# Decoder step on eight cores: first bands built during the x load, scores of the next unit ahead of each attention unit, other places for cache and output loads

## The chip, the cores and the metric

The kernel runs on the 8 cores of one Trainium2 chip. Each core has five engines that run their own instruction streams and wait for each other through semaphores: TensorE (PE, matmuls), VectorE (DVE), ScalarE (ACT), GpSimd (POOL) and SyncE (SP, which here only issues DMAs). All eight cores run one program on their own part of the data, without exchange. The time of a run is that of the slowest core, in device microseconds; the lower the better.

## The reference

One layer of a hybrid decoder, for a prompt of 4 x 2048 positions and 32 single decode positions, model width 2048:

```python
h = rms_norm(x, norm_mix_g);  z = h @ w_in       # q 1024 | k 256 | v 256 | GLU value 1024 | GLU gate 1024
q, k = rope(rms_norm(q)), rope(rms_norm(k))      # 16 query heads, 4 key/value heads of 64
a = attention(q, k, v, window 128, sink per head) # 128-blocks: own and previous key block; decode: cache
u = u_val * sigmoid(u_gate)                       # GLU
c = silu(layer_norm(causal_dwconv(u, width 31)))  # per channel; layer_norm over 1024 channels
x = x + concat([a, c]) @ w_out
x = x + square(relu(rms_norm(x) @ w_up)) @ w_down # hidden 8192
# returned beside x: the last keys, values and GLU rows of prompt and decode (caches shifted by one)
```

## The kernel before, in words

Each core has half a prompt (1024 positions, plus a halo of 128 for keys and convolution) and 4 decode positions. Everything is held transposed: channels on the 128 partitions, positions along the row. `Prog.add` keeps one instruction list per engine in the order of the calls and derives the semaphore waits from overlapping byte ranges and PSUM banks. So the order of the Python calls is the order on every engine, and each engine works strictly in that order. A DMA issued on POOL or SP also stands in that engine's list: its wait holds up all behind it.

**x load** (loop at L611). 16 chunks of x (`xu`, SP queue) come in; DVE scales each with the norm's gain into bf16 (`HT`, L612), ACT squares it, PE multiplies it with the first two weight blocks (gate and value of channel block 0) and sums the squares. The weights of the u projection (`load_wu`, 4 slots) come over POOL's queue.

**u blocks** (loop L835, c = 1 to 7). Per channel block of 128: `u_block` twice (gate in PSUM banks 0 to 2, value in 3 to 5, 48 matmuls each), `glu_gate` (DVE product, ACT sigmoid, POOL product with the norm), `glu_mul` (16 pieces on DVE, L681, into `UP`), `conv` (36 matmuls with banded matrices `BD`, banks 6 and 7, drained by ACT in 16 pieces, L706, into `CC`). `build_bands` (L657) makes the banded matrices from the taps `WT` on POOL, one product of 4608 columns per block, in two buffers. In the gaps, `kv_tile` projects a tile of keys and values (bank 6), chain1 and chain2 do norm and rotation on DVE, ACT and POOL, and `kv_tr` transposes the keys. For block 0, glu_mul's both inputs lie in SBUF, for the others one lies in PSUM.

**Passage** (from L1050). Last key tiles, q projection of the decode tile (9) and of tiles 1 and 2, the conv states (`u_outputs`, L868), the cache loads (`CKB`, `CVB`, L1064), and the first LayerNorm sums (`ln_cast`, `ln_stats`). In memory, the squares of `ln_cast` lie over the buffer `UTO` from which the conv state is sent out.

**Attention** (loop L1097, 8 blocks of 128 positions, two units of 8 heads each). `sc`: scores and mask, 8 matmuls in a ring of three banks, exps on ACT into `PT`; `pv`: sums and values, 8 matmuls in banks 7 and 6; `unit_b`: DVE adds the sink, ACT does Ln and Exp for the reciprocal, DVE multiplies. Between them stand quarters of the q projection three tiles ahead (`q_part`, banks 0 and 1), its norm and rotation (`q_chain1`, `q_chain2`), its transposes (`q_tr`), and the LayerNorm (`ln_norm1`, `ln_norm2`, per channel block: two DVE products of 1029 columns, then ACT's scaling of 1029 columns, L919). Sigmoids (`ln_sig`) and products (`ln_mul`) follow in blocks 5 and 6; each `ln_mul` is followed by the load of the residual chunk that goes into the same place.

**Output projection** (L1166 on) and **MLP** (64 hidden blocks): 16 output blocks of 48 matmuls, then groups of four up and 16 down blocks. Weights come over POOL's queue.

## Time and profile before

| | us |
|---|---|
| median of 3 runs | 1601.51 (1598.77 to 1603.36) |
| profiled execution | 1603.6 |
| its span, slowest core (core 7) | 1602.0 |
| spans of the eight cores | 1596.6 to 1602.0 |
| PE busy | 1406.0 (88% of the span) |
| DVE, ACT, POOL busy | 662.8, 389.3, 284.1 |

The share of PE is a mean over stages that differ: the page's 40 slices of 40 us show PE at nine tenths or more from slice 15 on and between five and seven tenths in most slices before, apart from slices 4 to 6. The clock of PE that the chip granted is full in the first and falls in the second. In the rows below, a line of the timeline gives the start, the length, the engine and line, and in brackets how long the engine stood idle before it and what ended that; xN means N instructions of this form in a row.

### The profile page before, as it was taken

Reading aid. Unit: us, or ns where it says so; the run is one execution under the profiler, and the core shown is the slowest. Engines: PE = TensorE matmul, PEld = TensorE weight load, DVE = VectorE, ACT = ScalarE, POOL = GpSimd, SP = SyncE. Lnnn points to the kernel's source line nnn. Section 1 sums busy time; section 2 is a strip of 40 time slices with the busy share of each in tenths; the row PEclk is TensorE's granted clock in tenths of the full one; section 3 lists DMA queues with packets and bytes.
Section 4 is the critical chain, followed back from the end, with each engine's and each line's share of the span. In section 5 each row is a group of like instructions: output and inputs, shape, how many; then the busy total and the mean of one; then the engine's idle time right before and its main releaser. Section 6 shows DMA issues by size and latency. Waiting matters only on the chain.

```text
span 1602.0 us, 22075 instructions; the slowest of 8 cores (1596.6 to 1602.0 us)
## 1 busy us (share of the span) xinstructions
PE 1406.0 (88%) x9006; PEld 869.2 (54%) x9006; DVE 662.8 (41%) x743; ACT 389.3 (24%) x536; POOL 284.1 (18%) x275
## 2 busy tenths in 40 slices
PE   5659997577655499999999999999999999999994
PEld 2436663222221366566666666666666666666663
DVE  2635555343433211115435435534443553453463
ACT  4256775154437122210100110010011011001000
POOL 0376652311211000010101110110010111011000
PEclk9879998778777799999999999999999999999997
DMA  9813431300001844484552553364355246336419
GB/s 253 161 27 53 81 60 39 32 26 0 1 0 53 208 77 71 68 137 73 92 81 45 86 92 55 65 106 67 53 92 91 44 78 99 58 62 100 66 35 177
DMA packets 52517, 122.75 MB, mean 77 GB/s; under 512 B 19215, under 2 KB 22543, under 8 KB 52395
## 3 DMA queue, kind: packets, MB, share of 16 engines
q0 software_dynamic: 43888, 91.07, 36.1%
q1 hardware_dynamic: 8531, 30.28, 7.0%
q8 instruction: 73, 1.20, 0.3%
q14 instruction: 25, 0.20, 0.0%
HBM read 203.42 MB, written 10.35 MB: 133 GB/s over the span
## 4 chain that ended last, share of the span: by engine, by line
PE 78%; DVE 5%; ACT 5%; DMA 4%; issue 3%; POOL 2%; SPq 1%; ACTq 0%; DVEq 0%; POOLq 0%
PE psum L535 78%; DVE arena L507 3%; ACT arena L503 3%; DMA arena<-cv 2%; DMA arena<-xu 2%; SPq L490 1%; POOL arena L507 1%; DVE arena L681 1%; DMA arena<-wo 1%; ACT L503 1%; ACT arena L706 0%; PE psum L539 0%; POOL arena L490 0%; POOL arena L522 0%; DVE arena L702 0%
## 5 line engine op out<-in xcount | busy, mean ns | idle before, releaser
L535 PE MATMUL psum<-arena 128*128 128x343 bf16 (+5 forms) x8880 | 1396.5, 320 | 147.5 <-ACT arena L503 86.2
L535 PEld LDWEIGHTS psum<-arena 128*128 128x128 bf16 (+1 forms) x8880 | 859.3, 99 | 676.0 <-issue 229.8
L507 DVE TENSOR_TENSOR arena<-psum,arena 128x1029 f32<-128x1029 f32 (+6 forms) x394 | 399.5, 1025 | 485.6 <-PE psum L535 420.3
L503 ACT ACTIVATE arena<-psum 128x1029 bf16<-128x1029 f32 (+6 forms) x157 | 117.5, 772 | 797.5 <-PE psum L535 790.2
L507 DVE TENSOR_TENSOR arena<-arena 128x1029 bf16<-128x1029 bf16 (+5 forms) x126 | 129.0, 1029 | 294.6 <-ACT arena L503 288.2
L507 POOL TENSOR_TENSOR arena<-arena 128x256 f32<-128x256 f32 (+7 forms) x74 | 172.8, 2338 | 408.7 <-DVE arena L507 164.9
L503 ACT ACTIVATE arena<-arena 128x1029 bf16<-128x1029 f32 (+13 forms) x201 | 142.0, 732 | 243.3 <-DVE arena L507 144.1
L681 DVE TENSOR_TENSOR arena<-psum,arena 32x264 bf16<-32x264 f32 x112 | 68.7, 614 | 73.2 <-PE psum L535 64.7
L490 POOL DMA_DIRECT2D arena<-wdn x64 | 34.2, 535 | 336.6 <-PE psum L535 333.7
L490 POOL DMA_DIRECT2D arena<-wup x64 | 34.8, 545 | 312.5 <-PE psum L535 312.5
L706 ACT ACTIVATE arena<-psum,arena 32x256 f32<-32x256 f32 x120 | 85.5, 712 | 4.5 <-PE psum L535 1.1
L539 PE MATMUL psum<-arena 128*128 128x128 bf16 (+5 forms) x126 | 13.0, 240 | 27.2 <-POOL arena L522 18.0
L503 ACT ACT_TABLE_LOAD x21 | 26.9, 1283 | 22.5 <-DVE arena L507 16.6
L539 PEld LDWEIGHTS psum<-arena 128*128 128x128 bf16 (+5 forms) x126 | 10.0, 114 | 35.2 <-issue 33.7
L612 DVE TENSOR_SCALAR arena<-arena 128x1060 bf16<-128x1060 f32 (+3 forms) x21 | 14.6, 693 | 34.7 <-DMA arena<-xu 34.0
L563 POOL DMA_DIRECT2D arena<-wo x16 | 8.6, 538 | 104.4 <-PE psum L535 103.8
L521 ACT COPY arena<-psum 128x256 bf16<-128x256 bf16 (+7 forms) x23 | 14.9, 652 | 47.9 <-PE psum L539 39.8
L681 DVE TENSOR_TENSOR arena<-arena 32x264 bf16<-32x264 f32 x16 | 17.5, 1096 | 5.6 <-POOL arena L507 5.1
L528 DVE TENSOR_REDUCE arena<-arena 128x4 f32<-128x256 bf16 (+4 forms) x20 | 16.1, 806 | 0.1
L563 POOL DMA_DIRECT2D arena<-wu x16 | 9.4, 589 | 36.3 <-DMA arena<-xu 35.4
L503 ACT ACTIVATE arena<-psum,arena 128x256 bf16<-128x256 f32 (+3 forms) x12 | 5.5, 472 | 19.6 <-DVE arena L507 19.6
L522 DVE CAST arena<-arena 128x343 bf16<-128x343 f32 (+2 forms) x29 | 9.6, 402 | 0.0
(16 smaller groups left out, 38.5 us busy)
## 6 DMA issues: line engine op xcount, KB each, us to landing
arena<-wup POOLq DMA_DIRECT2D x64, 512.0 KB, 7.7
arena<-wdn POOLq DMA_DIRECT2D x64, 512.0 KB, 9.7
arena<-xu SPq DMA_DIRECT2D x16, 530.0 KB, 21.6
arena<-xt SPq DMA_DIRECT2D x16, 514.0 KB, 10.2
yt<-arena SPq DMA_DIRECT2D x16, 514.0 KB, 14.1
arena<-wu POOLq DMA_DIRECT2D x16, 512.0 KB, 7.2
arena<-wo POOLq DMA_DIRECT2D x16, 512.0 KB, 6.2
arena<-wq POOLq DMA_DIRECT2D x16, 256.0 KB, 8.6
```

Of the source, the lines that this page charges most:

```text
L490: return P.add(eng, lambda e: e.dma_start(out=out.ap, in_=in_.ap), reads=[in_], writes=[out], key=key, group=group, final=final)
L503: return P.add("act", lambda e: e.activation(out=out.ap, in_=in_.ap, func=func, bias=b, scale=s), reads=rd, writes=[out])
L507: return P.add(eng, lambda e: e.tensor_tensor(out=out.ap, in0=in0.ap, in1=in1.ap, op=op), reads=[in0, in1], writes=[out])
L521: return P.add("act", lambda e: e.copy(out=out.ap, in_=in_.ap), reads=[in_], writes=[out])
L522: return P.add(eng, lambda e: e.tensor_copy(out=out.ap, in_=in_.ap), reads=[in_], writes=[out])
L528: return P.add("dve", lambda e: e.tensor_reduce(out=out.ap, in_=in_.ap, axis=AX.X, op=ALU.add), reads=[in_], writes=[out])
L535: return P.add("pe", lambda e: e.matmul(out.ap, lhsT.ap, rhs.ap, start=start, stop=stop), reads=[lhsT, rhs], writes=[out])
L539: return P.add("pe", lambda e: e.transpose(out.ap, in_.ap, ident.ap), reads=[in_, ident], writes=[out])
L563: P.add("pool", lambda e: e.dma_start(out=out.ap, in_=src_ap.rearrange("p (k m) -> p k m", m=m)), writes=[out], key="%s%d" % (tag, i), aft ...
L612: return P.add(eng, lambda e: e.tensor_scalar(out=out.ap, in0=in_.ap, scalar1=a1, scalar2=None, op0=op0), reads=rd, writes=[out])
L681: P.add("dve", (lambda o_=o_, i0=i0, i1=i1: (lambda e: e.tensor_tensor(out=o_.ap.rearrange("p (a t) -> p a t", t=88), in0=i0.ap, in1=i1.ap ...
L706: P.add("act", (lambda o_=o_, i_=i_, cb=cb: (lambda e: e.activation(out=o_.ap, in_=i_.ap, func=AF.Identity, bias=cb.ap, scale=1.0)))(), re ...
```

## The change

- The band of block 0 gets a buffer of its own (`BD0`, over the key and value buffers `KT` and `VT`, not yet in use) and is built on POOL during the x load. For this the 32-column identity and the conv bias come as a small load of their own (`cs2`), and the taps in two loads, block 0's first.
- The second gate product of block 0 runs on DVE instead of POOL. Key tile 0 moves behind the u gate block of c = 2, after conv(0); the gate product of block 1 moves ahead of the halo product; the query tables move from c = 1 to c = 2.
- The cache loads move from the passage into the u blocks (c = 3 and 4), into the buffer of the halo tile; the buffer `A2` of the q chain moves to the place they had. The one-row copies into `CVB` move to unit 2, the cache-to-cache copies to unit 9.
- In the passage, `u_outputs` moves behind the q projection of tile 1, `ln_cast(0)` and `ln_stats(0)` further back.
- In attention, the loop goes over units: the scores of unit u+1 (in two halves, with quarters of the q projection between) come before `pv` of unit u; `unit_b` is split in two around a LayerNorm step.
- The LayerNorm's gain and bias go into the sigmoid's scale and bias on ACT, and into a DVE instruction in `ln_mul`.
- The first three output weights are loaded at unit 11, the others after the block that frees their slot. The residual is loaded with its last column of zeros from the host instead of a memset.

```diff
-    CKB = sb(O_TAB + 5120, BF16, (SPC, 256))
-    CVB = sb(O_TAB + 7168, BF16, (SPC, 256))
+    CKB = sb(O_HH, BF16, (SPC, 256))
+    CVB = sb(O_HH + 2048, BF16, (SPC, 256))
...
+    BD0 = sb(O_KT, BF16, (4, 9, 128))
...
+    dma("sp", CS2(), R(cs2_d), "cs2")
+    dma("pool", WT((0, 144)), R(wt_d[:, 0:144]), "wt")
     xl = [dma("sp", XS(kc), R(xu_d[kc]), "xu%d" % kc) for kc in range(16)]
     dma("sp", CST(), R(cst_d), "cst")
     dma("sp", XTH(), R(xh_d.rearrange("k p t -> p k t")), "xh")
     dma("sp", TABIN(), R(tab_d.rearrange("p (a b c) -> p a b c", a=2, b=10)), "tab")
-    dma("pool", WT(), R(wt_d), "wt")
-    load_wu(after=[xl[10]])
-    load_wu(after=[xl[13]])
     memset("dve", ONB(), 1.0)
     memset("dve", ONM(), 1.0 / 1024.0)
     memset("dve", ONE1(), 1.0)
-    memset("pool", VT(9), 0.0)
+    cp("dve", ID32(), CS2((0, 32)))
+    cp("dve", CBP(), CS2((32, 64)))
     act(ESK(), SKT, AF.Exp)
+
+    def build_bands(c):
+        o_ = BD0() if c == 0 else BD[c % 2]()
+        w_ = WT((144 * c, 144 * c + 144))
+        tt("pool", Ref(o_.ap.rearrange("p a b (s q) -> p (a b s) q", q=32), o_.rngs),
+           bc(w_, 2, (128, 144, 32)), bc(ID32(), 1, (128, 144, 32)), ALU.mult)
+
+    build_bands(0)
+    load_wu(after=[xl[10]])
+    load_wu(after=[xl[13]])
+    dma("pool", WT((144, 1152)), R(wt_d[:, 144:1152]), "wt2")
...
-        tt("pool", SG(), SG(), RS(), ALU.mult)
+        tt("dve" if c == 0 else "pool", SG(), SG(), RS(), ALU.mult)
...
-    qb.A2 = sb(O_HH, F32, (16, 64))
+    qb.A2 = sb(O_TAB + 5120, F32, (16, 64))
...
-    for k4 in range(2):
-        load_wkv(k4)
+    load_wkv(0)
+    load_wu()
+    load_wkv(1)
     load_wu()
     load_wkv(2)
-    load_wu()
     load_wkv(3)
     glu_gate(0, ag)
-    build_bands(0)
+    act(SQH(), XTH(), AF.Square)
     glu_mul(0, av, 0)
     glu_mul(0, av, 1)
-    halo_norm()
     for c in range(1, 8):
-        if c >= 2:
+        if c >= 3:
             glu_mul(c - 1, acc3(1), 0)
             kv_tile(c - 2, 6)
             glu_mul(c - 1, acc3(1), 1)
+            if c == 3:
+                kv_tr(0, 7)
         u_block(pending.pop(0), acc3(0))
         if c == 1:
             halo_stats()
+        if c >= 3:
+            kv_tr(c - 2, 7)
+        if c == 2:
+            glu_mul(1, acc3(1), 0)
+            glu_mul(1, acc3(1), 1)
+            kv_tile(0, 6)
+        glu_gate(c, acc3(0))
+        if c == 1:
+            halo_norm()
             col_stats()
-        else:
-            kv_tr(c - 2, 7)
-        glu_gate(c, acc3(0))
         load_wu()
         if c == 1:
             tt("pool", GCK(), TABIN(0), bc(GK, 1, (128, 10, 64)), ALU.mult)
             tt("pool", GSK(), TABIN(1), bc(GKS, 1, (128, 10, 64)), ALU.mult)
-        conv(c - 1) if c >= 2 else None
-        if c == 1:
             build_bands(1)
-        elif c + 1 < 8:
-            build_bands(c + 1) if c >= 2 else None
+        else:
+            conv(c - 1)
+            if c + 1 < 8:
+                build_bands(c + 1)
         u_block(pending.pop(0), acc3(1))
         if c == 1:
             conv(0)
+            memset("dve", VT(9), 0.0)
             build_bands(2)
+        if c == 2:
             tt("pool", GCQ(), TABIN(0), bc(GQ, 1, (128, 10, 64)), ALU.mult)
             tt("pool", GSQ(), TABIN(1), bc(GQS, 1, (128, 10, 64)), ALU.mult)
         load_wu()
+        if c == 3:
+            dma("pool", CKB(p=(0, 127)), R(ck[:, 1:128, :].rearrange("s k d -> k s d")), "ckb")
+        if c == 4:
+            dma("pool", CVB(p=(0, 127)), R(cv[:, 1:128, :].rearrange("s k d -> k s d")), "cvb")
...
-        act(CC(c), CC(c), AF.Identity, scale=LG(c), bias=LB(c))
 
     def ln_sig(c):
-        act(SGL[c % 4](), CC(c), AF.Sigmoid)
+        act(SGL[c % 4](), CC(c), AF.Sigmoid, scale=LG(c), bias=LB(c))
 
     def ln_mul(c):
+        tscal("dve", CC(c), CC(c), LG(c), LB(c), ALU.mult, ALU.add)
         tt("dve", CT(c), CC(c), SGL[c % 4](), ALU.mult)
-        dma("sp", XT(c, (0, NX)), R(xt_d[c]), "xr%d" % c)
+        dma("sp", XT(c), R(xt_d[c]), "xr%d" % c)
...
-    def sc(ui):
+    def sc(ui, kb):
         n, gp = units[ui]
         own_c0 = MC0 + 128 * n
         cs = (gp * 4, gp * 4 + 4)
-        for kb, kc0 in enumerate((own_c0 - 128, own_c0)):
+        kc0 = own_c0 - 128 + 128 * kb
...
+    def unit_b1(ui):
         n, gp = units[ui]
-        own_c0 = 128 * n
         cs = (gp * 4, gp * 4 + 4)
-        pso = ps_f32(6, 1, (4, 128))
-        psd = ps_f32(7, 1, (4, 128))
-        rec = REC
-        tt("dve", rec(), psd(), bc(ESK(cs), 2, (128, 4, 128)), ALU.add)
-        act(rec(), rec(), AF.Ln)
-        act(rec(), rec(), AF.Exp, scale=-1.0)
-        tt("dve", AT(cs, (own_c0, own_c0 + 128)), pso(), rec(), ALU.mult)
+        tt("dve", REC(), ps_f32(7, 1, (4, 128))(), bc(ESK(cs), 2, (128, 4, 128)), ALU.add)
+        act(REC(), REC(), AF.Ln)
+        act(REC(), REC(), AF.Exp, scale=-1.0)
+
+    def unit_b2(ui):
+        n, gp = units[ui]
+        cs = (gp * 4, gp * 4 + 4)
+        tt("dve", AT(cs, (128 * n, 128 * n + 128)), ps_f32(6, 1, (4, 128))(), REC(), ALU.mult)
...
     kv_tile(9, 1)
+    q_part(9, 3, 0, 16)
     kv_tr(8, 2)
+    kv_tr(9, 2)
     dma("sp", R(nkp), KF_L(), "kvout", group=True, final=True)
     dma("sp", R(nvp), VF_L(), "kvout", group=True, final=True)
-    q_part(9, 3, 0, 16)
-    kv_tr(9, 2)
     dma("sp", R(nks[:, 127, :]), KF_S(p=(0, SPC)), "kvout", group=True, final=True)
     dma("sp", R(nvs[:, 127, :]), VF_S(p=(0, SPC)), "kvout", group=True, final=True)
-    dma("pool", CKB(p=(0, 127)), R(ck[:, 1:128, :].rearrange("s k d -> k s d")), "cks", group=True)
-    dma("pool", CVB(p=(0, 127)), R(cv[:, 1:128, :].rearrange("s k d -> k s d")), "cks", group=True)
-    for s_ in range(SPC):
-        dma("sp", CVB(s_, p=(127, 128)), VB_S(p=(s_, s_ + 1)), "cvs", group=True)
     q_chain1(9)
     q_chain2(9)
-    u_outputs()
     q_part(1, 0, 0, 16)
     q_tr(9)
     q_chain1(1)
-    ln_cast(0)
+    u_outputs()
     q_chain2(1)
     q_part(2, 3, 0, 16)
-    ln_stats(0)
+    ln_cast(0)
     q_tr(1)
     q_chain1(2)
+    memset("dve", QT((0, 8), (NM - 1, NM)), 0.0)
+    memset("dve", AT((0, 8), (NM - 1, NM)), 0.0)
+    ln_stats(0)
     ln_cast(1)
-    memset("pool", QT((0, 8), (NM - 1, NM)), 0.0)
-    memset("pool", AT((0, 8), (NM - 1, NM)), 0.0)
-    dma("sp", R(nks[:, 0:127, :]), R(ck[:, 1:128, :]), "d2d", group=True, final=True)
-    dma("sp", R(nvs[:, 0:127, :]), R(cv[:, 1:128, :]), "d2d", group=True, final=True)
-    dma("sp", R(ncs[:, 0:29, :]), R(scv[:, 1:30, :]), "d2d", group=True, final=True)
+    q_chain2(2)
 
...
+    wo_pend = []
+    for u in range(-1, 16):
+        qi = (u + 1) // 2 + 3
+        qh = (u + 1) % 2
+        qn = qi if qi <= 8 else None
+        if u + 1 < 16:
+            sc(u + 1, 0)
         if qn:
+            q_part(qn, 0, 8 * qh, 8 * qh + 4)
+        if u + 1 < 16:
+            sc(u + 1, 1)
+        if qn:
+            q_part(qn, 0, 8 * qh + 4, 8 * qh + 8)
+        if u == -1:
             ln_stats(1)
+            q_tr(2)
             ln_cast(2)
+        if u >= 0:
+            pv(u)
+            unit_b1(u)
+            if u >= 1:
+                ln_step()
+            unit_b2(u)
+            if u == 0:
+                ln_stats(2)
+            if u >= 1:
+                ln_step()
+        if qn and qh == 1:
             q_chain1(qn)
+        if qh == 0 and 4 <= qi <= 9:
+            q_chain2(qi - 1)
+        if qh == 1 and 4 <= qi <= 9:
+            q_tr(qi - 1)
+        if u == 2:
+            for s_ in range(SPC):
+                dma("sp", CVB(s_, p=(127, 128)), VB_S(p=(s_, s_ + 1)), "cvs", group=True)
+        if u == 4:
             samp_k()
+        if u == 6:
             samp_s()
+        if u == 8:
             samp_pv()
+        if u == 9:
             for c in range(4):
                 ln_sig(c)
+        if u == 11:
+            wo_pend += [wload(WSO, wo_d[i], "wso") for i in range(3)]
+        if u in (11, 12):
+            for c in (2 * (u - 11), 2 * (u - 11) + 1):
                 ln_mul(c)
+        if u == 12:
             for c in range(4, 8):
                 ln_sig(c)
+        if u in (13, 14):
+            for c in (4 + 2 * (u - 13), 5 + 2 * (u - 13)):
+                ln_mul(c)
+        if u == 9:
+            dma("sp", R(nks[:, 0:127, :]), R(ck[:, 1:128, :]), "d2d", group=True, final=True)
+            dma("sp", R(nvs[:, 0:127, :]), R(cv[:, 1:128, :]), "d2d", group=True, final=True)
+            dma("sp", R(ncs[:, 0:29, :]), R(scv[:, 1:30, :]), "d2d", group=True, final=True)
...
-    pending = [wload(WSO, wo_d[0], "wso"), wload(WSO, wo_d[1], "wso")]
+    pending = wo_pend
     for dc in range(16):
         w = pending.pop(0)
-        if dc + 2 < 16:
-            pending.append(wload(WSO, wo_d[dc + 2], "wso"))
         accb = acc3(next_slot())
         for kc in range(16):
             kk = korder[kc]
             src = AT if kk < 8 else CT
             for pi, (a, b) in enumerate(PM):
                 mm(accb(pi, (0, 343)), w(kk), src(kk % 8, (a, b)), kc == 0, kc == 15)
+        if dc + 3 < 16:
+            pending.append(wload(WSO, wo_d[dc + 3], "wso"))
```

POOL's list from the taps' load on, before (`wt` taps, `wu` u weights, `wkv` key/value weights; 128x4608 is a band, 128x1060 a gate product; k_xu10 is the landing of x chunk 10):

```order
L490 DMA arena<-wt 128x1152
L563 DMA arena<-wu 128x2048 [waits k_xu10]
L563 DMA arena<-wu 128x2048 [waits k_xu13]
L532 MEMSET arena 128x256
L490 DMA arena<-wkv 128x4x512 [waits k_cst,s_dve]
L490 DMA arena<-wkv 128x4x512
L563 DMA arena<-wu 128x2048 [waits s_pe,k_wsu0]
L490 DMA arena<-wkv 128x4x512
L563 DMA arena<-wu 128x2048 [waits s_pe,k_wsu1]
L490 DMA arena<-wkv 128x4x512
L507 TENSOR_TENSOR arena<-arena 128x1060 [waits s_act]
L507 TENSOR_TENSOR arena<-arena 128x4608 [waits k_xu11,k_xu9,k_wt]
```

and after:

```order
L492 DMA arena<-wt 128x144
L509 TENSOR_TENSOR arena<-arena 128x4608 [waits s_dve,k_wt]
L565 DMA arena<-wu 128x2048 [waits k_xu10]
L565 DMA arena<-wu 128x2048 [waits k_xu13]
L492 DMA arena<-wt 128x1008
L492 DMA arena<-wkv 128x4x512 [waits s_dve,k_cst,k_cs2]
L565 DMA arena<-wu 128x2048 [waits s_pe,k_wsu0]
L492 DMA arena<-wkv 128x4x512
L565 DMA arena<-wu 128x2048 [waits s_pe,k_wsu1]
L492 DMA arena<-wkv 128x4x512 x2
L509 TENSOR_TENSOR arena<-arena 128x1060 [waits s_act]
```

The band of block 0 has moved from behind the first gate product to ahead of two weight loads, and that gate product is gone from POOL.

ACT's list in attention, one unit, before (psum 128x512 are exps of scores, 128x512 in SBUF Ln and Exp of the reciprocal, 128x16 the q norm, 128x8x128 the copy of transposed queries, 128x1029 the LayerNorm scaling):

```order
L503 ACTIVATE arena<-arena 128x512 [waits s_dve]
L503 ACTIVATE arena<-arena 128x512 [waits s_act]
L503 ACTIVATE arena<-arena 128x1029 [waits s_dve]
L503 ACTIVATE arena<-psum 128x512 [waits s_pe] x4
L521 COPY arena<-psum 128x8x128 [waits s_pe]
L503 ACTIVATE arena<-arena 128x512 [waits s_dve]
L503 ACTIVATE arena<-arena 128x512 [waits s_act]
```

and after:

```order
L505 ACTIVATE arena<-psum 128x512 [waits s_pe] x4
L505 ACTIVATE arena<-arena 128x512 [waits s_dve]
L505 ACTIVATE arena<-arena 128x512 [waits s_act]
L505 ACTIVATE arena<-arena 128x16 [waits s_pool]
L505 ACTIVATE arena<-arena 128x16 [waits s_act]
L505 ACTIVATE arena<-psum 128x512 [waits s_pe] x4
L505 ACTIVATE arena<-arena 128x512 [waits s_dve]
L505 ACTIVATE arena<-arena 128x512 [waits s_act]
```

Between Exp of a unit and the next exps of scores the 128x1029 scaling, which waits for DVE, no longer stands.

SP's list in the passage, before (nks, nvs, ncs, ncp are outputs; the copies 1x16x16 fill the last row of `CVB`):

```order
L490 DMA nks<-arena 4x256 [waits s_pool]
L490 DMA nvs<-arena 4x256 [waits s_act]
L490 DMA arena<-arena 1x16x16 [waits k_cks]
L490 DMA arena<-arena 1x16x16 x3
L490 DMA ncp<-arena 32x1024 [waits s_act]
L490 DMA ncs<-arena 4x1024
L490 DMA nks<-ck 4x2x16256
```

and after:

```order
L492 DMA nks<-arena 4x256 [waits s_pool]
L492 DMA nvs<-arena 4x256 [waits s_act]
L492 DMA ncp<-arena 32x1024 [waits s_act]
L492 DMA ncs<-arena 4x1024
L492 DMA arena<-arena 1x16x16 [waits k_cvb]
L492 DMA arena<-arena 1x16x16 x3
L492 DMA nks<-ck 4x2x16256
```

The state outputs ncp and ncs have moved ahead of the copies, and the copies wait for another load (k_cvb).

## Rows read from the trace of the kernel before

**Rows 1.** Stretches of core 7: from:to us, then busy us of each engine.
```profile
48.00:113.00 65.00, 39.88 (x248) 23.71 (x248) 37.75 (x61) 26.94 (x40) 41.41 (x20) 0.82 0.49 83
113.00:247.00 134.00, 132.56 (x868) 84.70 (x866) 68.18 (x130) 98.04 (x140) 75.56 (x50) 0.98 0.42 71
247.00:327.00 80.00, 45.04 (x221) 21.21 (x220) 34.53 (x61) 27.00 (x60) 25.26 (x18) 0.76 0.20 29
...
356.70:492.40 135.70, 85.79 (x416) 30.77 (x416) 55.28 (x63) 63.81 (x100) 23.58 (x11) 0.78 0.00 0
492.40:542.00 49.60, 17.82 (x67) 4.98 (x67) 14.65 (x16) 20.61 (x32) 3.75 (x5) 0.64 0.43 117
542.00:1540.00 998.00, 994.39 (x6687) 654.68 (x6688) 397.72 (x345) 118.87 (x116) 106.76 (x157) 1.00 0.48 79
```

**Rows 2.** Waits of PE up to 560 us: who, releaser, total us, times, longest.
```profile
PE psum L535 <- ACT arena L503: 82.8, 19, 15.3
PE psum L535 <- DMA arena<-wo: 20.6, 1, 20.6
```

**Rows 3.** Timeline of the start-up: start us, us, engine, line, operation, idle before.
```profile
57.44 10.30 POOL L507 TENSOR_TENSOR arena<-arena 128x1060 f32<-128x1060 f32 x2 [1.34 <-ACT arena L503]
59.98 8.25 DVE L681 TENSOR_TENSOR arena<-arena 32x264 bf16<-32x264 f32 x1 [5.15 <-POOL arena L507]
...
78.02 2.47 DVE L507 TENSOR_TENSOR arena<-arena 128x32 f32<-128x32 f32 x3
...
88.29 21.76 POOL L507 TENSOR_TENSOR arena<-arena 128x640 f32<-128x640 f32 x6
...
112.80 0.37 PE L539 MATMUL psum<-arena 128*128 128x128 bf16 x2 [9.00 <-POOL arena L522]
```

**Rows 4.** Groups by form, 0 to 542 us: busy us, mean ns, idle before it.
```profile
L681 DVE TENSOR_TENSOR arena<-psum,arena 32x264 bf16<-32x264 f32 x112 | 68.7, 614 | 73.2 <-PE psum L535 64.7 <-POOL arena L507 5.2
L507 POOL TENSOR_TENSOR arena<-arena 128x4608 bf16<-128x4608 bf16 x8 | 63.2, 7906 | 1.0 <-PE psum L535 0.9
...
L507 POOL TENSOR_TENSOR arena<-arena 128x1060 f32<-128x1060 f32 x8 | 19.4, 2429 | 52.6 <-ACT arena L503 28.4 <-PE psum L535 24.1
...
L612 DVE TENSOR_SCALAR arena<-arena 128x1060 bf16<-128x1060 f32 x16 | 12.4, 772 | 34.0 <-DMA arena<-xu 34.0
...
L503 ACT ACTIVATE arena<-arena 128x1029 f32<-128x1029 f32 x8 | 10.0, 1246 | 26.9 <-DVE arena L507 26.9
...
L521 ACT COPY arena<-psum 128x1024 bf16<-128x1024 bf16 x8 | 8.2, 1020 | 16.1 <-PE psum L539 16.1
...
L507 DVE TENSOR_TENSOR arena<-arena 128x1060 f32<-128x1060 f32 x1 | 1.3, 1265 | 2.2 <-ACT arena L503 2.2
```

**Rows 5.** Timeline of the passage after the u blocks.
```profile
275.03 1.49 PE L539 MATMUL psum<-arena 4*128 4x4 bf16 x10 [3.44 <-POOL arena L522]
...
283.48 8.30 PE L535 MATMUL psum<-arena 128*128 128x512 bf16 x32
...
310.25 2.50 SPq L490 DMA_DIRECT2D arena<-arena  x4
...
315.59 3.65 ACT L503 ACTIVATE arena<-arena 128x343 bf16<-128x343 f32 x10 [22.04 <-DMA ncs<-arena]
```

**Rows 6.** DMA issues: KB each, median us from issue to landing.
```profile
arena<-cv POOLq DMA_DIRECT2D x1, 254.0 KB, 30.2
```

**Rows 7.** Timeline of a unit of block 3 in attention.
```profile
404.25 2.42 DVE L507 TENSOR_TENSOR arena<-psum,arena 128x1024 f32<-128x1024 f32 x3 [2.42 <-ACT arena L503]
...
405.62 8.17 PE L535 MATMUL psum<-arena 64*128 64x512 bf16 x32 [5.43 <-ACT arena L503]
...
411.26 1.35 ACT L503 ACTIVATE arena<-arena 128x512 f32<-128x512 f32 x2 [2.70 <-DVE arena L507]
...
413.32 2.56 DVE L507 TENSOR_TENSOR arena<-arena 128x1029 f32<-128x1029 f32 x2
```

**Rows 8.** Timeline of attention: PE's run in block 1 after short waits.
```profile
358.79 5.89 PE L535 MATMUL psum<-arena 128*128 128x512 bf16 x29 [1.12 <-DVE arena L507]
```

103 lines of the change are left out of this document (29 added, 74 removed).

## The prediction, made before the changed kernel ran

> **What bounds the kernel now.** I read the stretches first, then who TensorE (PE) waits for, then the timeline of three places. The stretches [rows 1] cut the 1602.0 us span by what is computed. From 542 us (output projection and MLP) PE is busy 994.39 of 998.00 us at clock 1.00; nothing of the change reaches that part except by moving its start. The blocks of the u projection, 113 to 247 us, are full too (132.56 of 134). The loss lies in three other stretches: start-up 48 to 113 us (PE 39.88 of 65 us), the passage 247 to 327 us (45.04 of 80), attention (85.79 of 135.70, and 17.82 of the 49.60 us up to the projection), at mean clocks of 0.64 to 0.82. What PE waits for there: ScalarE (ACT), 82.8 us in 19 waits, and once the first output weights, 20.6 us [rows 2]. So each microsecond by which the output projection starts earlier should come off the time. The sum is made against the profiled execution, 1603.6 us by its own clock (1.6 us beside the span), 2.1 us over the median 1601.51.
>
> **Start-up, term 1.** Before, GpSimd (POOL) multiplies the first gate and then builds band 0, 10.30 us in two instructions from 57.44 [rows 3]. The first of 16 band inputs (line 681) on VectorE (DVE) starts at 59.98 and takes 8.25 us; the same piece with an operand in PSUM takes 614 ns [rows 3, 4]. So the DVE instruction with both inputs in SBUF stands still as long as POOL's runs, and the pieces, the halo product behind them (78.02, in the 2.47 us) and the small copies of column statistics that free PSUM bank 7 all come late. Then POOL works 21.76 us in one go (four table products, bands 1 and 2), and PE waits 9.00 us at 112.80 for POOL's cast of the first keys [rows 3].
> After: band 0 is built during the x load, the first gate product goes to DVE: 57.4 + 1.27 = 58.7; 16 pieces at 0.614 end at 68.5; two small ones, the next gate product (about 1.4) and the halo product (about 2.3) bring the copies to about 73.4, where they were at 80.4. The sigmoid of block 1 lies beside the halo product and ends there too; POOL's 2.43 us product ends at 75.8, 16 pieces at 0.614 at about 86.3 (they read PSUM, so POOL doesn't hold them). POOL has meanwhile done two tables and band 1 (2 x 1.5 + 7.9, at 87.3), the key tile's own drain ends at about 88.7, and there conv(1) can start, where before it started at 113. The transposes of key tile 0 no longer stand in front. That is 24 us. Given back: band 2, band 3 and two tables now stand on POOL ahead of the second key tile (about 114 in the new count), and its transposes come right after a u block that ends at 112: 1 to 2 us. Term 1: -23. Bounds: -10 if the freed wait only moves to the key tile's transposes (PE's 9.00 us wait gone, little else), -27 if nothing waits.
> Hidden edits here. Band 0 takes 7.9 us on POOL at about 19 to 27 us, when the first taps have landed, and can hold up one of the 16 scalings of x (0.77 us each). These idle 34.0 us for x [rows 4], so the backlog of five is worked off before the last chunk; if that cover fails, up to 7.9 us are lost. The Trainium skill ("SBUF — State Buffer", section "Who interferes with whom") says that a VectorE instruction with two SBUF inputs is blocked for the whole of a GpSimd instruction that reads SBUF, and that tensor_scalar can be blocked too. The trace agrees with the first half, 8.25 us against 0.614. For the scalings no row here shows it; by the rule the stall comes, without it nothing does, and the sum is the same as long as x is what ends the stage. The small constants load is issued ahead of x, the rest of the taps behind the fourth weight: same bytes, other order, counted 0 (bounds -2 to +2). DVE's cast of these constants now waits ahead of all scalings; the 34.0 us cover it.
>
> **Passage, term 2.** Before, POOL issues the cache loads at 275 to 285, the second lands 30.2 us after its issue [rows 6]. SP waits for it, and only at 310.25 can it copy the last value row and then issue the state outputs; ACT, whose squares overwrite the buffer of these outputs, is idle 22.04 us until 315.59 [rows 5]. The transposes of keys at 275.03 and the projection at 283.48 have the state transposes between them: 8.2 us after 275.3 [rows 5]. After: the loads are issued in the u blocks, where PE is full and POOL is busy 75.56 of 134 us [rows 1], two blocks and more ahead of use; the outputs no longer queue behind the copy (SP order below the diff); the projection follows the key transposes at once. Gained: 22.0 + 8.2. Given back: the state transposes, copies and row sums now stand ahead of the LayerNorm casts on ACT and DVE, and ACT's squares of the second and third column group stand ahead of the first exps: about 4. Term 2: -26; bounds -15 (the wait alone, a third of it refilled) and -31.
>
> **Attention, term 3.** Five pairs of units (blocks 1 to 5) take 135.70 us [rows 1], 27.1 each, sample attention included. In such a pair PE needs 64 matmuls of 512 columns, at 5.89/29 = 0.203 us [rows 8] 13.0 us, and 0.6 of transposes. The rest is a ring: the exps of the next scores stand on ACT behind the LayerNorm scaling, which itself waits for two DVE products (413.32, 2.56 us); over the eight scalings ACT works 10.0 us and stands idle 26.9 [rows 4, 7]. After: the scaling goes into the sigmoid and into DVE, later; scores of unit u+1 come before the sums of u, so PE has the projection's 16 matmuls and the scores under the Ln/Exp of 1.35 us [rows 7]. What is late next: once a pair, the new queries must be transposed and copied by ACT (behind Ln/Exp, a square of 1024 columns and the copy itself, 1.02 [rows 4]) before the next scores: PE idle 2.7 us. And the query bank is free only after DVE's reciprocal product (512 columns, about 0.7 beside 1.28 for the 1029 of a LayerNorm product), one such LayerNorm product and the 2.42 us of rotary products [rows 7]: 1.5 more. 13.6 + 4.2 = 17.8; restarts after a wait run at the low clock, as 405.62 shows (8.17 us for 32 matmuls, 0.255 each [rows 7]), so I take 20. Sample attention and four sigmoids add about 12 over the five. 5 x 20 + 12 = 112. Term 3: -24; bounds -5 (ring still closed) and -45 (18 a pair, nothing added).
>
> **The end of attention, term 4.** 49.60 us [rows 1], of which PE waits 20.6 for the first output weights, issued only after the last DVE product [rows 2]. After: they are issued four units before the end. Left is 29.0; I add 3.6, since eight DVE scalings of about 0.8 to 1.0 come into the last five units. So 32.6. Term 4: -17; bounds -10 and -25. The first residual loads come earlier too and find their use later than their landing: 0.
>
> Sum: -23 - 26 - 24 - 17 = -90, so 1513.6 by the profile's own time, and 1511.5 by the median. The projection's first matmul moves from 542 to about 452.
>
> **Rivals.**
> Fuller: the pairs run at 18 and the tail keeps nothing of the old waits: -23 - 26 - 45 - 25 = -119, about 1482. For it: PE's idle in these stretches adds up to over 140 us; against: the query copy still stands in the loop.
> Weaker: the scores do not really lead, because ACT and DVE work in order: an exp behind an Ln that waits for a sum keeps the ring closed, and the wait that left start-up returns at the key transposes. -10 - 18 - 12 - 12 = -52, about 1549. For it: 82.8 us of waits for ACT, most of whose work stays. Against: 36.9 us of ACT time and idleness do go.
> No change: the stretches before 542 are refilled altogether. Against it: the 20.6 us and 22.0 us waits are for single DMAs whose issue moves by tens of microseconds.
> Slower: one mechanism could do it, the clock of the long dense part. It is 1.00 over 998 us now [rows 1]; if denser work ahead of it made the chip grant the low level there, each microsecond at half speed costs half, so more than 180 us at the low level would eat the 90. Over 1606 us then. For it: only that the clock does move in this kernel; against: it falls only around waits, and the dense part holds 1.00 throughout.
>
> **How the numbers follow.** Forecast 1512 (1490 to 1535): 0.54. Fuller: 0.17. Weaker: 0.23. No change within 0.3% (4.8 us, about what such a measurement can tell): 0.02. Slower: 0.04. The range takes in the fuller case's own value and reaches past the weaker one: 1480 to 1560. Faster: 0.94.
>
> **What would show it.** Right: the first matmul of conv(1) at about 89 instead of 113; no ACT idle of over 5 us behind the state outputs; PE waits for ACT under 50 us in total; mean period of a pair near 22 with sample attention; the projection's first matmul about 452 and no wait for its weights. Wrong: scalings of x that end later than 48 us; POOL's casts named as PE's releaser for more than a few microseconds; a granted clock under 0.98 in the dense part.

## The result, and the profile after

The changed kernel takes 1541.91 us in the median of four runs (1531.83 to 1738.76), the kernel before 1601.38; the ratio is 0.960, 95% interval 0.953 to 0.967. Runs in which the cores of one die showed a lower granted clock (here 1738.76 us, at 0.80 to 0.81) stand in the medians but not in the ratios, nor in the single times given below. The profiled execution took 1533.42 us against 1603.6 before: 70.2 us less, where the forecast was 90.

By stretches (view of windows, core 4: from:to, length, then busy us and count of PE, PE's weight loads, DVE, ACT, POOL, then PE's clock, DMA share, GB/s), cut at the same events as [rows 1]: conv(1) starts, the u blocks end, first scores, scores of unit 2, of unit 12, output projection:

```profile
48.00:88.50 40.50, 33.08 (x246) 21.55 (x247) 31.28 (x60) 26.75 (x39) 19.71 (x12) 0.99 0.84 135
88.50:236.50 148.00, 135.79 (x862) 87.03 (x868) 68.85 (x132) 98.25 (x141) 96.26 (x59) 0.93 0.49 68
236.50:289.50 53.00, 40.99 (x219) 20.34 (x221) 30.36 (x58) 23.16 (x50) 16.34 (x16) 0.94 0.07 24
289.50:324.00 34.50, 22.65 (x94) 9.47 (x96) 9.54 (x28) 16.08 (x36) 4.25 (x2) 0.80 0.05 22
324.00:438.10 114.10, 80.21 (x409) 29.92 (x417) 56.32 (x62) 55.69 (x94) 23.39 (x10) 0.85 0.00 1
438.10:475.80 37.70, 21.64 (x80) 5.49 (x80) 22.30 (x26) 22.04 (x33) 6.00 (x5) 0.65 0.53 126
475.80:1473.80 998.00, 993.29 (x6665) 654.27 (x6679) 401.22 (x349) 120.10 (x118) 107.07 (x157) 1.00 0.47 80
```

Start-up, passage, the five blocks and the tail are shorter, the dense part is the same (993.29 of 998 us busy at clock 1.00). One of the stretches shown before is longer: the u blocks, 148.0 us instead of 134. PE's busy time there has grown by only 3 us (135.79 against 132.56), so most of the loss is idle time. Who PE waits for between 48 and 560 us (view of waits: total us, times, longest), against [rows 2]:

```profile
PE psum L537 <- ACT arena L505: 31.9, 11, 7.5
PE psum L537 <- DVE arena L509: 20.6, 8, 5.0
PE psum L541 <- POOL arena L524: 19.7, 6, 8.8
PE psum L537 <- ACT arena L523: 11.7, 4, 4.4
```

The wait for output weights is gone and ACT's 82.8 us (then line 503) have become 31.9, with 11.7 for its copies. POOL's casts (line 524) have not gone down. Before, they had this row:

```profile
PE psum L539 <- POOL arena L522: 18.0, 7, 9.0
```

Only its longest wait has moved. The 9.00 us ahead of the first key transposes [rows 3] have become 0.31, but inside the u blocks, where no such wait was over 0.5 us before, there are now one of 2.61 and one of 8.79. The prediction had named POOL's casts as PE's releaser for more than a few microseconds as a sign that it was wrong.

To compare kernels by stage (the runs e1 to e12 are explained below), I measured the same events on all eight cores of each profiled run and took the median of the cores: start to the first drain of conv(1) by ACT; to the first band input of block 7 on DVE (u blocks); to the first exponential of unit 0 (passage), of unit 2, of unit 12 (five blocks); to the residual sum of the first output chunk (tail).

| us | to conv(1) | u blocks | passage | units 0, 1 | five blocks | tail | rest |
|---|---|---|---|---|---|---|---|
| before | 116.9 | 122.9 | 88.3 | 27.7 | 135.7 | 59.3 | 1046.5 |
| changed | 92.2 | 135.2 | 67.3 | 29.7 | 111.7 | 46.4 | 1046.0 |
| e1: cache loads of 128 rows | 90.5 | 125.4 | 67.7 | 29.7 | 111.6 | 46.6 | 1046.4 |
| e2: value cache load later | 91.3 | 127.1 | 66.4 | 29.9 | 111.7 | 46.5 | 1046.8 |
| e3: cache loads back in the passage | 91.5 | 123.3 | 76.2 | 29.5 | 114.6 | 46.6 | 1046.6 |
| e4: band 0 late | 100.2 | 144.4 | 66.5 | 30.3 | 111.5 | 46.6 | 1045.0 |
| e5: no lead | 92.3 | 134.4 | 67.3 | 39.4 | 111.3 | 38.7 | 1048.0 |
| e6: exponential for the sigmoid | 91.4 | 134.4 | 67.4 | 29.8 | 108.6 | 43.5 | 1047.3 |
| e7: output weights late | 92.0 | 134.4 | 67.2 | 30.0 | 111.4 | 46.6 | 1045.9 |
| e8: queries early | 91.0 | 134.5 | 67.3 | 29.8 | 112.0 | 46.0 | 1046.9 |
| e9: memset back | 91.9 | 134.8 | 67.7 | 29.7 | 111.2 | 63.8 | 1045.6 |
| e10: scale on ACT | 91.6 | 134.8 | 67.7 | 29.7 | 139.2 | 42.4 | 1045.6 |
| e11: scale on ACT, no lead | 91.0 | 135.0 | 67.4 | 42.6 | 144.5 | 34.2 | 1045.8 |
| e12: together | 91.3 | 124.5 | 68.1 | 30.4 | 113.0 | 45.6 | 1046.4 |

Without the lead, units 0 to 2 and 12 stand elsewhere in the order, so for those rows the last three stages are to be read as a sum.

### The profile page after: what moved, and what is told of

The parts are those of the page before. It is cut to its first block, busy times and chain, and to the rows that moved or that the text cites. A ratio compares the mean times of both kernels' runs of the same rounds, so it can differ in the third digit from the quotient of the medians.

```text
span 1531.9 us, 22004 instructions; the slowest of 8 cores (1525.7 to 1531.9 us)
## 1 busy us (share of the span) xinstructions
PE 1394.6 (91%) x8970; PEld 868.5 (57%) x9006; DVE 670.1 (44%) x755; ACT 380.0 (25%) x528; POOL 284.6 (19%) x271
## 4 chain that ended last, share of the span: by engine, by line
PE 85%; ACT 4%; DVE 3%; issue 3%; POOL 2%; DMA 1%; SPq 0%; DVEq 0%; ACTq 0%; POOLq 0%
PE psum L537 85%; ACT arena L505 3%; DVE arena L509 2%; DMA arena<-xu 1%; POOL arena L509 1%; DVE arena L626 1%; ACT L505 1%; ACT arena L523 0%; ACT arena L712 0%; PE psum L541 0%; DVE arena L708 0%; POOL arena L492 0%; DVE arena L628 0%; DVE arena L687 0%; POOL arena L524 0%
## 5 line engine op out<-in xcount | busy, mean ns | idle before, releaser
L537 PE MATMUL psum<-arena 128*128 128x343 bf16 (+7 forms) x8844 | 1385.2, 320 | 94.7 <-ACT arena L505 35.5
L509 DVE TENSOR_TENSOR arena<-psum,arena 128x1029 f32<-128x1029 f32 (+5 forms) x394 | 399.6, 1025 | 421.5 <-PE psum L537 390.1
L509 DVE TENSOR_TENSOR arena<-arena 128x1029 bf16<-128x1029 bf16 (+5 forms) x127 | 132.2, 1041 | 297.0 <-ACT arena L505 290.9
L505 ACT ACTIVATE arena<-arena 128x1029 bf16<-128x1029 f32 (+12 forms) x193 | 132.8, 717 | 175.2 <-DVE arena L509 112.9
L541 PE MATMUL psum<-arena 128*128 128x128 bf16 (+5 forms) x126 | 11.9, 228 | 26.5 <-POOL arena L524 19.7
L626 DVE TENSOR_SCALAR arena<-arena 128x1060 bf16<-128x1060 f32 (+3 forms) x21 | 21.3, 1040 | 25.8 <-DMA arena<-xu 23.6
L687 DVE TENSOR_TENSOR arena<-arena 32x264 bf16<-32x264 f32 x16 | 10.0, 627 | 0.6
L524 DVE COPY arena<-psum 128x343 f32<-128x343 f32 (+4 forms) x7 | 3.1, 463 | 13.7 <-PE psum L537 13.7
## 6 DMA issues: line engine op xcount, KB each, us to landing
arena<-wu POOLq DMA_DIRECT2D x16, 512.0 KB, 10.9
```

Source lines behind the costliest of these rows:

```text
L505: return P.add("act", lambda e: e.activation(out=out.ap, in_=in_.ap, func=func, bias=b, scale=s), reads=rd, writes=[out])
L509: return P.add(eng, lambda e: e.tensor_tensor(out=out.ap, in0=in0.ap, in1=in1.ap, op=op), reads=[in0, in1], writes=[out])
L524: return P.add(eng, lambda e: e.tensor_copy(out=out.ap, in_=in_.ap), reads=[in_], writes=[out])
L537: return P.add("pe", lambda e: e.matmul(out.ap, lhsT.ap, rhs.ap, start=start, stop=stop), reads=[lhsT, rhs], writes=[out])
L541: return P.add("pe", lambda e: e.transpose(out.ap, in_.ap, ident.ap), reads=[in_, ident], writes=[out])
L626: return P.add(eng, lambda e: e.tensor_scalar(out=out.ap, in0=in_.ap, scalar1=a1, scalar2=None, op0=op0), reads=rd, writes=[out])
```

## The experiments

Ratios are to the kernel before, run on the same chip beside the changed one. "Lands" means that a load's data have arrived.

**Where the u blocks lost 12 us.** Timeline of the changed kernel there, core 4 (start, duration, engine, operation, in brackets the idle time before and who ended it):

```profile
130.19 4.57 POOL L492 DMA_DIRECT2D arena<-ck  x1
...
162.87 4.58 POOL L492 DMA_DIRECT2D arena<-cv  x1 [9.54 <-issue]
167.43 1.63 POOL L492 DMA_DIRECT2D arena<-wq  x3
...
170.76 0.40 POOL L524 CAST arena<-arena 128x256 bf16<-128x256 f32 x1
...
171.30 0.37 PE L541 MATMUL psum<-arena 128*128 128x128 bf16 x2 [8.79 <-POOL arena L524]
```

POOL stands still for 9.54 us in front of the second cache load, then issues for 4.58 us, and only then come the products and the cast for which PE's transposes of the keys wait. The view of DMA issues (KB, us from issue to landing) shows when the first load landed: 130.19 + 32.1 = 162.3, 0.6 us before the second one's issue starts. All eight cores show the same 0.6 us.

```profile
arena<-ck POOLq DMA_DIRECT2D x1, 254.0 KB, 32.1
arena<-cv POOLq DMA_DIRECT2D x1, 254.0 KB, 32.8
```

*e1_rows128:* all 128 rows are loaded, so 128 partitions; order does not matter to a softmax sum, and the new row takes the place of row 0. The transposes of the cached keys then take 128 rows too (not shown).

```diff
-dma("pool", CKB(p=(0, 127)), R(ck[:, 1:128, :].rearrange("s k d -> k s d")), "ckb")
+dma("pool", CKB(), R(ck.rearrange("s k d -> k s d")), "ckb")
...
-dma("pool", CVB(p=(0, 127)), R(cv[:, 1:128, :].rearrange("s k d -> k s d")), "cvb")
+dma("pool", CVB(), R(cv.rearrange("s k d -> k s d")), "cvb")
...
-cp("dve", Ref(KTS.ap[:, :, :, 127], KTS().rngs), Ref(ktn.ap.rearrange("p c s -> p s c"), ktn.rngs))
+cp("dve", Ref(KTS.ap[:, :, :, 0], KTS().rngs), Ref(ktn.ap.rearrange("p c s -> p s c"), ktn.rngs))
...
-dma("sp", CVB(s_, p=(127, 128)), VB_S(p=(s_, s_ + 1)), "cvs", group=True)
+dma("sp", CVB(s_, p=(0, 1)), VB_S(p=(s_, s_ + 1)), "cvs", group=True)
```

> The cache loads take all 128 rows (128 partitions) instead of rows 1 to 127; the new key or value then overwrites row 0 instead of filling row 127. Theory: in the changed kernel GpSimd's issue of the second cache load (162.87 us) starts 0.6 us after the first has landed, and the landing takes 32 us because a load on 127 partitions breaks into thousands of 4-byte packets; with 128 partitions it lands in about 10 us and is issued in about 1 us, GpSimd's 9.5 us gap goes, PE's waits for the key casts (2.61 + 8.79 us) fall under 2 us together, the u blocks take 136 us instead of 148, and the time falls by 11 to 14 us, to about 1520. Rival: the slow landing and issue come from the 512-byte rows and the cast, not from the count of partitions: landing stays over 25 us, the gap stays, time within 3 us of 1532.

Measured: 1523.69 us (1521.98 to 1526.95), ratio 0.953 (0.950 to 0.956). u blocks 125.4 us. Timeline and landings on core 4:

```profile
127.85 0.76 POOL L492 DMA_DIRECT2D arena<-ck  x1
...
151.37 0.76 POOL L492 DMA_DIRECT2D arena<-cv  x1
```

```profile
arena<-ck POOLq DMA_DIRECT2D x1, 256.0 KB, 6.7
arena<-cv POOLq DMA_DIRECT2D x1, 256.0 KB, 7.3
```

One row more, and issue falls from 4.57 to 0.76 us, landing from 32 to 7. The page's count of packets falls with it, from the changed kernel's line to this kernel's:

```profile
DMA packets 52805, 122.76 MB, mean 80 GB/s; under 512 B 19503, under 2 KB 22959, under 8 KB 52683
```

```profile
DMA packets 37573, 122.70 MB, mean 80 GB/s; under 512 B 4263, under 2 KB 7727, under 8 KB 37451
```

15,240 small packets less, so the two loads of 127 rows made some 7,620 each. The theory holds; the gain is 8 to 10 us rather than the 11 to 14 expected.

*e2_cv_late:* `if c == 4` becomes `if c == 6` for the value cache load.

> Only the issue of the value cache load moves, from block c = 4 to c = 6; both loads stay at 127 partitions. Theory (the second load's issue waits for the first one's landing): at c = 6, about 40 us later, the first has long landed, so there is no gap on GpSimd; PE's 8.79 us wait at the third key tile falls under 1 us, and the 4.6 us of the issue itself costs 2 to 4 us of wait at a later key tile. Time down by 5 to 8 us, about 1525. Rival (the value load is slow to issue by itself, whatever stands ahead): the gap of 7 to 10 us moves with it to c = 6 and PE waits there; time within 3 us of 1532.

Measured: 1524.06 us, ratio 0.953 (0.950 to 0.956), u blocks 127.1. The load comes at 198.09 without a gap, the first one having landed at about 159 (129.14 + 29.7):

```profile
187.84 10.30 POOL L509 TENSOR_TENSOR arena<-arena 128x1060 f32<-128x1060 f32 x2 [6.00 <-PE psum L537]
198.09 4.64 POOL L492 DMA_DIRECT2D arena<-cv  x1
```

The load still takes 4.64 us to issue, but the gap did not move with it: the gap belongs to a second such load behind one still under way. The theory holds.

*e3_loads_back:* both loads move to the place just ahead of `q_chain1(9)`.

> Both cache loads go back to the passage (behind the last key tile, ahead of the first query tile's products), as in the kernel before; everything else as in the changed kernel. Theory (issuing them in the u blocks costs 12 us there): u blocks 136 us instead of 148; the passage pays for 9.2 us of issue on GpSimd in front of the products of the query tiles, 4 to 9 us; nobody waits for the landing, since the outputs no longer queue behind it and unit 4 is 70 us away. Time down by 3 to 8 us, 1524 to 1529. Rival (the step as the forecast had it, free in the u blocks): the passage loses 9 us and nothing comes back, about 1541.

Measured: 1533.53 us, ratio 0.959 (0.955 to 0.962): no faster than the changed kernel, though the rival's 1541 did not come either. The u blocks give back the 12 us (123.3), the passage takes 8.9 (76.2), with PE waiting for the products that stand behind the two issues:

```profile
252.88 4.63 POOL L492 DMA_DIRECT2D arena<-ck  x1 [0.54 <-issue]
257.49 4.56 POOL L492 DMA_DIRECT2D arena<-cv  x1
...
266.58 2.17 PE L541 MATMUL psum<-arena 4*128 4x4 bf16 x16 [5.21 <-POOL arena L509]
```

Its 114.6 us in the five blocks come from four cores whose mean clock is 0.71 there (117.8 us; 111 on the others, at 0.85); that takes back the 3 us left. Moving these loads was thus worth less than nothing as it was done: 8.9 us won in the passage, 12 lost in the u blocks.

**Start-up.** *e4_band0_late:* `build_bands(0)` stands behind `glu_gate(0, ag)` again.

> Band 0 is built where it was before, on GpSimd behind the first gate, instead of during the x load; the gate product stays on DVE and the rest as in the changed kernel. Theory (DVE stands still while GpSimd works on SBUF): the first of the 16 band inputs takes about 8 us instead of 0.6, conv(1) starts 7 to 10 us later than 88.5, time up by 7 to 10 us, about 1541. Rival (the start-up gain came from the order of work alone, with band 0 hidden either way): conv(1) within 3 us of 88.5, time within 3 us of 1532.

Measured: 1551.33 us, ratio 0.970 (0.967 to 0.973); conv(1) is drained at 100.2 instead of 92.2. Timeline, core 7:

```profile
55.99 7.97 POOL L509 TENSOR_TENSOR arena<-arena 128x4608 bf16<-128x4608 bf16 x1
...
57.87 7.22 DVE L509 TENSOR_TENSOR arena<-arena 128x1060 f32<-128x1060 f32 x1 [2.56 <-ACT arena L505]
```

The gate product, 1.26 us in the changed kernel, now takes 7.22: it begins while POOL works and ends after POOL has. The theory holds, though the instruction that stands still is this product and not the first band input, as it said. So 8.0 of the 25 us of the start-up are band 0's; the start-up's other edits were not undone one by one. About 10 us more of this run lie in the u blocks (144.4 on the median core). They go with a lower granted clock: on the two cores without it the u blocks take 134.7 and 136.6 us, as in the changed kernel (last section).

**The five blocks.** *e5_no_lead:* per unit, `q_part` of 8, then `pv(u)`, `unit_b1`, `unit_b2`, LayerNorm steps, and only then `sc(u + 1, 0); sc(u + 1, 1)`.

> In the changed kernel only the lead is undone: the scores of unit u+1 come behind the sums and the LayerNorm steps of unit u, and the 8 projection matmuls of a unit stand together ahead of the sums. Theory (the lead itself opened the ring): the five blocks from the scores of unit 2 to those of unit 12, 111.8 us in the changed kernel and 136 before, go back to 128 to 140, the last units lose 3 to 6 more, time about 1550 to 1560. Rival (the gain came from ScalarE's eight scalings that went into the sigmoid, 10.0 us busy and 26.9 idle): the five blocks stay within 6 us of 111.8, time under 1540.

Measured: 1534.02 and 1541.28 us, ratio 0.961 (0.957 to 0.965). From the first exponentials to the first output chunk 189.4 us (39.4 + 111.3 + 38.7), with the lead 187.8. My theory falls and the rival holds: with the scaling off ACT, the lead is worth 1.6 us.

*e10_scale_on_act:* the scale and shift go back into an ACT instruction.

```diff
 tt("dve", c3(), c3(), RSL(), ALU.mult)
+act(CC(c), CC(c), AF.Identity, scale=LG(c), bias=LB(c))
...
-act(SGL[c % 4](), CC(c), AF.Sigmoid, scale=LG(c), bias=LB(c))
+act(SGL[c % 4](), CC(c), AF.Sigmoid)
...
-tscal("dve", CC(c), CC(c), LG(c), LB(c), ALU.mult, ALU.add)
```

> In the changed kernel only the LayerNorm's scale and shift go back to ScalarE (eight more instructions of 1.25 us behind the second LayerNorm product), out of the sigmoid and off DVE; the scores still lead. Theory (the run without the lead kept 111 us): ScalarE's place in the ring is what counts, and each scaling puts its 1.25 us and its wait for DVE ahead of the next exponentials; five blocks 122 to 136 us instead of 111.8, time up by 10 to 22, about 1546. Rival (with the lead there is room on ScalarE for them; either of the two edits would have done): five blocks within 5 us of 111.8, time under 1538.

Measured: 1555.40 us, ratio 0.972 (0.969 to 0.975); five blocks 139.2, all three stages 211.3: 23.5 us more than the 187.8 above, for eight instructions moved to ACT. Groups by form, core 4 (busy us, mean ns, idle before):

```profile
L505 ACT ACTIVATE arena<-arena 128x1029 f32<-128x1029 f32 x8 | 10.0, 1244 | 16.2 <-DVE arena L509 16.2
```

ACT works 10.0 us on them and stands 16.2 us in front of them waiting for DVE's product, with the next exponentials queued behind. The theory holds; its size is a little above what was expected (five blocks 139.2 against at most 136).

*e11_scale_no_lead:* both edits together.

> Both undone: scale and shift on ScalarE and the scores behind the sums; the rest of the loop (queries finished a unit earlier, LayerNorm steps spread, weights early) stays as changed. Theory (these two carry the gain of the blocks): five blocks 130 to 140 us, as the 136 of the kernel before. Rival (the gain comes from the finer order of the loop's other parts): under 120 us.

Measured: 1563.93 and 1566.40 us; three stages 221.4. With the scaling on ACT the lead is worth 10.1 us (221.4 to 211.3), without it 1.6: the two cover the same stall, and the scaling is the larger part. One thing more shows here: before, the three stages took 222.7 us, 20.6 of them waiting for output weights [rows 2], a wait that this run no longer has. So without these two edits the new loop is slower than the old one, by some 16 to 19 us (an estimate: 221.4 - 222.7 + 17.2, the cost of that wait in e9 below, or + 20.6). Which of its other edits costs that, no run shows.

*e6_exp_gate:* `AF.Exp` in place of `AF.Sigmoid` in `ln_sig`; the kernel then leaves out the sigmoid of the convolution branch, and only its time is read.

> The eight sigmoids of the convolution branch are replaced by exponentials of the same size, so that ScalarE needs no other function table there (the conv branch's values are then not the reference's). Theory: each group of four, 4.65 us with two table loads of 1.28, stands ahead of the next exponentials, and PE waits for it (7.46 and 5.76 us): without the four loads the five blocks fall by 2 to 4 us, the last units by 2 to 4, time down by 4 to 7, about 1527. Rival: DVE's products or the query copies end last there, and nothing moves by more than 2 us.

Measured: 1527.16 and 1528.33 us, ratio 0.955 (0.953 to 0.958); five blocks 108.6, tail 43.5: 6.0 us less together, as the theory had it. In the changed kernel one group of four sigmoids, its second table load and PE's wait behind it read:

```profile
421.63 4.65 ACT L505 ACTIVATE arena<-arena 128x1029 bf16<-128x1029 f32 x4
426.31 1.28 ACT L505 ACT_TABLE_LOAD   x1
...
428.34 5.54 PE L537 MATMUL psum<-arena 64*128 64x512 bf16 x18 [7.46 <-ACT arena L505]
```

*e8_queries_early:* `q_tr(qi - 1)` moves ahead of `pv(u)`.

> In the changed kernel the transposes of the next block's queries and their copy by ScalarE come ahead of the sums of the unit, not behind them. Theory (what bounds a pair of units now is the copy, which stands behind Ln, Exp and a square of 1024 columns): PE's waits for it, 16.7 us in 6 places, nearly go; five blocks 102 to 108 us instead of 111.8, last units 42 to 45 instead of 46.4, time down by 6 to 13, about 1523. Rival: the copy now delays Ln and Exp, so the sums' banks come free a microsecond later in each pair and the ring takes back what was won: within 3 us of 1532.

Measured: 1531.46 us, ratio 0.958 (0.956 to 0.960); five blocks 112.0, tail 46.0. The waits for the copy do vanish (0.7 us in two places are left), but those for ACT's other work and for DVE grow by 12.6 us together. The rival holds.

**The tail.** *e7_wo_late:* the first three `wload(WSO, ...)` move behind the loop.

> In the changed kernel only the first three output weight loads go back to the end of attention, behind the last product of the LayerNorm branch. Theory: their landing ends last again; from the scores of unit 12 to the first chunk's end it takes 56 to 64 us instead of 46.4, time up by 10 to 17, about 1546. Rival (the tail is bound by the last units' chain on ScalarE and DVE, the loads were hidden beside it): within 4 us of 1532.

Measured: 1533.11 us, ratio 0.958 (0.957 to 0.960); tail 46.6. The rival holds, but for another reason than it gave: POOL's list has nothing between the last query product and these loads, so they are issued as early as in the changed kernel, 8.2 us behind the first exponential of unit 12 against 8.1.

*e9_memset_back:* as e7, and `memset("pool", XT((0, 16), (NM - 1, NM)), 0.0)` stands in front of the loads again.

> As the run with late output weights, and in addition the residual's last column is again set to zero by GpSimd, ahead of the weight loads in its list, and no longer loaded. Theory: in the kernel before the loads were late because this memset stood in front of them and waited for the last LayerNorm product (31.61 us idle, then the memset at 529.02 and the loads at 529.71); with it back the stretch from the scores of unit 12 to the end of the first output chunk takes 56 to 64 us instead of 46.6, PE waits 10 us or more for the first output weights, time up by 10 to 17, about 1546. Rival (the loads come early enough either way, since the chain of the last units is the bound): the stretch stays within 3 us of 46.6.

Measured: 1549.42 us in one run; tail 63.8 on the median core, 17.2 more than in e7. In the kernel before, and then in this one:

```profile
529.02 0.13 POOL L532 MEMSET arena<- 128x16 f32 x1 [31.61 <-DVE arena L507]
529.71 1.72 POOL L563 DMA_DIRECT2D arena<-wo  x3 [0.56 <-issue]
```

```profile
482.18 0.12 POOL L534 MEMSET arena<- 128x16 f32 x1 [34.71 <-DVE arena L509]
482.69 1.67 POOL L565 DMA_DIRECT2D arena<-wo  x3 [0.39 <-issue]
...
494.31 5.95 PE L537 MATMUL psum<-arena 128*128 128x343 bf16 x27 [18.12 <-DMA arena<-wo]
```

A memset of 0.12 us, which must wait until DVE has read the last convolution values out of the same bytes, held the weights. Loading a zero column instead took it away.

**A faster version.** *e12_together:* e1 and e8, and `q_chain1` ahead of the second LayerNorm step.

> The changed kernel with cache loads of 128 rows, the next queries' transposes ahead of the sums, and the rotary products of a new query tile on DVE ahead of the second LayerNorm step of the unit instead of behind it. Theory: the first brings the 10 us already measured; the other two together take DVE's and the copy's waits out of a pair (1.7 to 1.9 us for the query bank, 3 for the copy), five blocks 102 to 108 us, time 1513 to 1519. Rival: the ring closes elsewhere as it did with the queries alone, blocks stay at 110 to 112, time 1521 to 1525.

Measured: 1523.21 us (1521.02 to 1539.05), ratio 0.953 (0.949 to 0.957): as e1 alone. Five blocks 113.0, so the rival holds. Both are faster than the changed kernel: their intervals at most touch those of e7 and e8, the two variants of it that changed nothing (0.957 to 0.960 and 0.956 to 0.960), and their u blocks take 125.4 and 124.5 us against 135.2. What closes the ring in the five blocks now is not settled.

## Why the prediction was right, and where it was not

The direction and the range held (1531.8 to 1550.4 us, within 1480 to 1560); the likeliest value was 20 us too low. The output projection starts at about 475.8 us, where about 452 was said. Term by term, from the table:

- **Start-up**, -23: measured -24.7. conv(1)'s first matmul comes at 88.51 (88.7 forecast). The band inputs run as priced, and the scalings of x do stall but catch up, as the step said: on the eight cores the last one ends at 46.9 to 48.6 us, before at 47.3 to 49.4.

```profile
19.93 7.90 POOL L509 TENSOR_TENSOR arena<-arena 128x4608 bf16<-128x4608 bf16 x1 [16.58 <-DMA arena<-wt]
20.09 13.26 DVE L626 TENSOR_SCALAR arena<-arena 128x1060 bf16<-128x1060 f32 x8 [1.83 <-DMA arena<-xu]
...
58.01 10.50 DVE L687 TENSOR_TENSOR arena<-arena 32x264 bf16<-32x264 f32 x16
...
88.51 17.67 PE L537 MATMUL psum<-arena 128*128 128x256 bf16 x99 [2.98 <-ACT arena L505]
```

- **The step that failed** stands in term 2: "the loads are issued in the u blocks, where PE is full and POOL is busy 75.56 of 134 us [rows 1], two blocks and more ahead of use". I looked at when the data is needed and at POOL's share of the stretch, not at what stands behind the two issues on POOL. [rows 6] showed a landing of 30.2 us and the issues take 4.6 us each; behind them in POOL's order stand the products of a key tile for which PE comes within microseconds. Cost: +12.3 us in the u blocks, where the sum had nothing; e1, e2 and e3 give back 9.8, 8.1 and 11.9 of them. It is the larger part of the miss of 20.
- **Passage**, -26: measured -21.0. ACT's idle time of 22.04 us [rows 5] is gone; the longest one between 265 and 300 us is 4.25. By e3, 8.9 us are the loads' issues leaving POOL; the other 12 are put down to the order of the state outputs by the trace alone, no run undid that part.
- **Five blocks**, -24 (112 us): measured 111.7. Right in size, in part by luck. The prediction gave the scaling and the lead together; e5 and e10 show that the scaling, once off ACT, leaves the lead 1.6 us. The 23.5 us hold for the changed loop; the old loop with only the scaling moved was not run. And of the waits from which the 112 was added up the largest, the query copy, was there (11.7 us) but does not set the time: e8 takes it out and stays at 112.0, and e12, with the products of a new query tile earlier as well, at 113.0.
- **Tail**, -17: measured -12.9. The wait for weights went. The prediction laid that to the earlier call of the loads. But without the memset the loads are as early with the late call (e7), and with the memset and the late call the wait is back (e9). So taking out the memset was enough, an edit that the prediction did not mention at all; whether the earlier call alone, ahead of the memset in POOL's list, would have been enough too was not run. What was left out of the sum is the second group of sigmoids with its table loads (about 3 us by e6).
- Units 0 and 1, not in the sum: +2.0, put down to the LayerNorm casts that left the passage; no run shows it. Dense part: clock 1.00 as before, so the slower rival did not come.

Sum: -24.7 + 12.3 - 21.0 + 2.0 - 24.0 - 12.9 - 0.5 = -68.8, from the medians of the cores. The "weaker" rival gave 1549 by a ring that stays closed; that was not it. Its other half, a wait that comes back at the key transposes, did come (8.79 us), though by the cache loads.

## What to carry to other kernels

When an instruction moves on an in-order engine, read what stands behind it in its new place and who waits for that; the engine's busy share there says nothing. When a load is late, look for the instruction in front of it in its queue before moving the load: here 0.1 us of memset held 17 us. Two edits that open the same stall can't be priced apart from one trace; undo each of them, alone and together.
